# Two inverse square roots per pair of heads on POOL, as a power, in a one-core transformer kernel

## The reference

```python
kk = (k * k_k).reshape(hd)
kk = kk * lax.rsqrt(jnp.maximum(jnp.sum(kk * kk, axis=-1, keepdims=True), 1e-24))
...
y = rwkv7_scan(r, decay, k, v, -kk, kk * a)
mu = jnp.mean(y, axis=-1, keepdims=True)
var = jnp.mean(jnp.square(y - mu), axis=-1, keepdims=True)
y = ((y - mu) * lax.rsqrt(var + GN_EPS)).reshape(bsz, s, c) * gn_w + gn_b
```

## Time and profile before

| what | value |
|---|---|
| median of 3 runs | 2821.63 us |
| profiled execution, and its span | 2820.33 us, 2818.5 us |
| PE (TensorE) busy | 2771.2 us, 98% |
| DVE (VectorE) busy | 2023.7 us, 72% |
| ACT (ScalarE) busy | 1364.0 us, 48% |
| POOL (GpSimd) busy | 479.3 us, 17% |
| TensorE clock granted | full speed in all 40 slices |
| DMA busy share | 50.3% of 16 engines |

### The profile page before, as it was taken

How to read it: one execution, slowest core, us unless ns; L and a number is a source line. 1 busy time by engine, 2 the same in 40 slices (tenths; PEclk the granted TensorE clock), 3 DMA queues, 4 the chain that set the end, 5 groups by cost and what they waited for, 6 DMA issues and landing times.

```text
span 2818.5 us, 42260 instructions
## 1 busy us (share of the span) xinstructions
PE 2771.2 (98%) x16660; PEld 2434.1 (86%) x16660; DVE 2023.7 (72%) x3102; ACT 1364.0 (48%) x2051; POOL 479.3 (17%) x526
## 2 busy tenths in 40 slices
PE   8999999999999999999999999999999999999998
PEld 7888888888888888888888888878998888888887
DVE  7987797776776666656657888878677777667655
ACT  6453455455555445434435545434454444444434
POOL 2211011110111111001102635421111111001101
PEclk9999999999999999999999999999999999999999
DMA  6444333455555555555556534221365555555555
GB/s 227 162 160 159 121 116 132 145 191 188 193 187 190 192 191 191 192 190 193 188 183 199 177 124 133 92 76 53 120 202 191 191 192 189 193 188 194 189 180 164
DMA packets 133396, 474.65 MB, mean 168 GB/s; under 512 B 14800, under 2 KB 15056, under 8 KB 132944
## 3 DMA queue, kind: packets, MB, share of 16 engines
q1 hardware_dynamic: 133200, 471.96, 50.3%
HBM read 469.80 MB, written 2.10 MB: 167 GB/s over the span
## 4 chain that ended last, share of the span: by engine, by line
PE 90%; DVE 5%; ACT 2%; POOL 1%; issue 1%; DMA 0%; SPq 0%; DVEq 0%; ACTq 0%; POOLq 0%
PE ps L899 90%; DVE U L1869 1%; DVE ringl L1869 1%; POOL U L2551 1%; ACT high L1409 1%; PE ps L902 1%; POOL U L2624 0%; ACT U L1409 0%; DVE U L1878 0%; DVE xT L1869 0%; DMA xT<-in_x_dram 0%; DVE hx L1869 0%; DVE U L2067 0%; ACT hr L1409 0%; DVE U L1875 0%
## 5 line engine op out<-in xcount | busy, mean ns | idle before, releaser
L899 PE MATMUL ps<-hr,high 128*128 128x512 f32 x4672 | 1491.4, 397 | 11.8 <-DVE ringl L1869 10.8
L1869 DVE TENSOR_TENSOR ringl<-ring,high 128x1024 fp32r<-128x1024 f32 x888 | 1082.6, 1221 | 435.1 <-ACT high L1409 434.6
L1409 ACT ACTIVATE high<-ring 128x1024 fp32r<-128x1024 f32 x888 | 915.6, 1033 | 601.6 <-PE ps L899 590.7
L899 PEld LDWEIGHTS ps<-hr,ringl 128*128 128x128 f32 x4672 | 879.2, 188 | 192.5 <-issue 1.4
L899 PE MATMUL ps<-hr,ringl 128*128 128x256 f32 x4672 | 924.3, 279 | 0.0
L899 PEld LDWEIGHTS ps<-hr,high 128*128 128x128 f32 x4672 | 717.6, 188 | 21.0 <-issue 15.1
L899 PE MATMUL ps<-yur,high 128*128 128x512 f32 (+1 forms) x2432 | 682.9, 370 | 3.8 <-DVE xT L1869 2.2
L2551 POOL TENSOR_TENSOR U<-U,rs 128x256 f32<-128x256 f32 x292 | 264.5, 906 | 1688.3 <-DVE U L1869 1668.8
L899 PEld LDWEIGHTS ps<-yur,ringl 128*128 128x128 f32 x2176 | 400.0, 188 | 79.6
L1409 ACT ACTIVATE U<-ps 128x256 f32<-128x256 f32 (+3 forms) x481 | 172.8, 371 | 592.0 <-PE ps L899 567.6
L899 PE MATMUL ps<-yur,ringl 128*128 128x256 f32 x2176 | 429.9, 279 | 0.0
(11 more groups left out here) (178 smaller groups left out, 1250.2 us busy)
## 6 DMA issues: line engine op xcount, KB each, us to landing
ring<-in_w_dram SPq DMA_DIRECT2D x862, 512.0 KB, 3.3
ring<-in_w_dram SPq DMA_DIRECT2D x48, 256.0 KB, 3.3
xT<-in_x_dram SPq DMA_DIRECT2D x3, 512.0 KB, 8.1
out_dram<-hx SPq DMA_DIRECT2D x3, 512.0 KB, 2.7
cst<-in_cst_dram SPq DMA_DIRECT2D x1, 1374.5 KB, 12.5
yT<-in_lora_dram SPq DMA_DIRECT2D x1, 1024.0 KB, 7.4
xT<-in_x_dram SPq DMA_DIRECT2D x2, 256.0 KB, 4.5
U<-in_lora_dram SPq DMA_DIRECT2D x1, 512.0 KB, 5.4
```

Source lines behind the costliest of these rows:

```text
L899: return e.matmul(out, l, r, start=start, stop=stop)
L1409: return e.activation(out, i, ACT.Copy, scale=scale)
L1869: return e.tensor_tensor(out, a, b, op)
```

## The change

For each of the two normalisations, ACT's square root and DVE's reciprocal are replaced by one POOL operation that raises the tile to the power in a tile of constants, all minus one half (`mhalf`, 256 columns more in the constants). Ahead of the recurrence POOL takes what DVE has written after the maximum. Behind it ACT still moves the variance out of PSUM with scale and epsilon, as an Identity in place of the square root, since POOL's power reads SBUF. The steps `kk`, `nrm`, `var` and `fin` get other engines and assumed times in `RECUR`.

```diff
-         ("kk", ("PE", 0.45), ("DVE", 0.42), ("ACT", 1.7)), ("nrm", ("DVE", 3.1)), ...
+         ("kk", ("PE", 0.45), ("DVE", 0.42), ("POOL", 2.0)), ("nrm", ("DVE", 1.35)), ...
-       ... ("var", ("PE", 0.45), ("ACT", 1.8)), ("fin", ("DVE", 2.2), ("+POOL", 2.9))]
+       ... ("var", ("PE", 0.45), ("ACT", 0.45), ("POOL", 2.0)), ("fin", ("DVE", 0.45), ("+POOL", 2.9))]
# constants
+        ("mhalf", 256), ("zero", 128), ("causal", 128), ("causalT", 128),
# ACT, rwkv
-                    e.wait_ge(vc_.sem, vc_.after("kk2", q))
-                    e.activation(E, E, ACT.Sqrt).then_inc(ac.sem, ac.inc("rk", q))
-                    yield "kk"
...
-                    e.activation(rs, ps[b][:, 0:256], ACT.Sqrt, scale=1.0 / 64, bias=C("eps64"))\
+                    e.activation(rs, ps[b][:, 0:256], ACT.Identity, scale=1.0 / 64, bias=C("eps64"))\
# DVE, rwkv
-                    e.wait_ge(ac.sem, ac.after("rk", q))
-                    e.reciprocal(E, E).then_inc(vc_.sem, vc_.inc())
-                    e.wait_ge(vc_.sem, vc_.last())
+                    e.wait_ge(qc.sem, qc.after("ik", q))
                     tt(KK, KK, E, MUL).then_inc(vc_.sem, vc_.inc("nrm", q))
...
-                    e.wait_ge(ac.sem, ac.after("rs", q))
-                    e.reciprocal(rs, rs).then_inc(vc_.sem, vc_.inc())
-                    e.wait_ge(vc_.sem, vc_.last())
+                    e.wait_ge(qc.sem, qc.after("ir", q))
# POOL, rwkv, between "dec" and "fin"
+                    e.wait_ge(vc_.sem, vc_.after("kk2", q))
+                    tt(w["E"], w["E"], C("mhalf"), ALU.pow).then_inc(qc.sem, qc.inc("ik", q))
+                    yield "kk"
+                    rs = w["XT"].rearrange("p a b -> p (a b)")[:, 0:256]
+                    e.wait_ge(ract[s].sem, ract[s].after("rs", q))
+                    tt(rs, rs, C("mhalf"), ALU.pow).then_inc(qc.sem, qc.inc("ir", q))
+                    yield "var"
```

More of the change, by code:

```diff
@@ L49 @@
 RECUR = [("lw", ("PE", 1.75), ("DVE", 0.9), ("ACT", 2.4)), ("dec", ("DVE", 1.9), ("+POOL", 4.8), ("ACT", 0.4)),
-         ("kk", ("PE", 0.45), ("DVE", 0.42), ("ACT", 1.7)), ("nrm", ("DVE", 3.1)), ("em", ("DVE", 1.2)), ("exp", ("ACT", 2.9)),
+         ("kk", ("PE", 0.45), ("DVE", 0.42), ("POOL", 2.0)), ("nrm", ("DVE", 1.35)), ("em", ("DVE", 1.2)), ("exp", ("ACT", 2.9)),
          ("rk", ("PE", 0.45), ("DVE", 0.42)), ("ar", ("DVE", 1.8)), ("rows", ("PE", 0.9), ("ACT", 1.1)),
@@ L54 @@
        ("G1", ("PE", 0.7), ("ACT", 0.35)), ("sa1", ("PE", 0.45), ("ACT", 0.45)), ("o1", ("PE", 1.1), ("ACT", 0.35)),
-       ("mean", ("PE", 0.45), ("DVE", 0.45), ("ACT", 0.45)), ("var", ("PE", 0.45), ("ACT", 1.8)), ("fin", ("DVE", 2.2), ("+POOL", 2.9))]
+       ("mean", ("PE", 0.45), ("DVE", 0.45), ("ACT", 0.45)), ("var", ("PE", 0.45), ("ACT", 0.45), ("POOL", 2.0)), ("fin", ("DVE", 0.45), ("+POOL", 2.9))]
 ROPE1 = (("DVE", 2.9),)
@@ L74, in layout @@
         ("ones", 128), ("norm1", 16), ("eps", 1), ("ident", 128), ("bones", 128), ("SU", 128), ("utri", 128), ("MC", 4 * 64), ("B8", 128), ("E8", 8),
-        ("zero", 128), ("causal", 128), ("causalT", 128),
+        ("mhalf", 256), ("zero", 128), ("causal", 128), ("causalT", 128),
         ("head", 2), ("R2", 128), ("cos1", 256), ("sin1", 256), ("inv2", 1), ("cmpmask", 32), ("anyv", 2),
@@ L2743, in constants @@
     put("anyv", np.stack([i >= 31, i >= 0], 1).astype(np.float32))
+    put("mhalf", np.full((128, 256), -0.5, np.float32))
     put("eps", np.full((128, 1), EPS, np.float32))
```

## The result

The changed kernel takes 3442.78 us, the median of four runs (3439.72 to 3444.68), beside 2822.93 us for the kernel before (four runs, 2818.89 to 2824.79). The ratio is 1.2198, with a 95% interval of 1.218 to 1.2217: 22% slower, where 2818 us was forecast and the range ended at 2870. One number further down needs a word: of the two runs of the kernel with 20 us in its table one took 3515.68 us, at a granted clock of 0.805 over its span where the other had 0.921, and it is left out.

What follows compares the result with a forecast made beforehand. PE, busy 98% of the span, was taken to bound the kernel. From 2820.3 us, 4.5 of PE's waits went and 1.0 for later multiplies came: 2816.8, carried to the median 2818 us; range 2808 to 2870.

Steps and rivals of the forecast that it cites:

- The size of the power: Each of sixteen 128x256 powers on POOL was taken as 2.0 us, between 0.6 and 3.8 us.
- B: Slow power: DVE stands in order at 16 places and splits for PE are late; 2871 us at 7.6 us; chance 0.24.
- B1: The same DVE waiting in small, with a power of 3.8 to 6 us: 2839 us at 5 us; chance 0.14.
- 12 us for each microsecond: Kernel time lost per microsecond of power, between 2825 us at 3.8 and 2871 at 7.6.
- the quarter for the second power: Behind the recurrence, only a quarter of the second chain's delay was counted, 9 us at a power of 7.6 us.
- The gain of 4.5 us: Three waits of PE with removed work directly ahead should go: 1.61 + 1.59 + 1.31 us; bounds 0 and 13.8.
- the redrawn order moves them about, and I count on none of it: The other 9.3 us of PE's waits, for the triangular inverse and copies out of PSUM, were counted as no gain.
- the wait at the end of the recurrence: At 2006.77 PE waits 1.59 us for an evacuation behind the last reciprocal on DVE; it should vanish.
- the next from 1.31: At 2011.15 PE waits 1.31 us more in the same chain, from the last y to its halves; it should vanish.
- the one of 1.61 at 1963: At 1962.99 PE waits 1.61 us for an evacuation on ACT behind a table load and a square root; counted as gain.
- the ceiling of 13.8 us: Sum of PE's waits in the recurrence's stretch, 0.5% of the time: all that shorter DVE or ACT work can give back.
- The constants' DMA: At the start, 131 KB more of constants take 1.2 us more to transfer; costed at nothing, 1.2 us if wrong.

Runs made afterwards that it cites:

- the kernel with 20 us in its table: The changed kernel with 20.0 in place of 2.0 us for both powers in the table from which the order is drawn: 3326.34 us, by one run.
- 1.7 us at each place: The changed kernel, same order and table, with two products by a constant tile in place of each power: 2836.06 us, ratio 1.0045.
- one product at each place: The changed kernel with one product by a constant tile in place of each power: 2835.11 us; with 0.9 us in the table 2829.11, with the old durations 2842.26.

## Why the prediction was wrong, step by step

1. **The size of the power is the step that failed**: "POOL's longest operation of this shape, with two arithmetic steps, is nearest ... so I take 2.0 us", with 3.8 as the upper bound. It is 41.3 us, alone as well as in place, eleven times the bound. The bound came from DVE's ratio of a reciprocal to a two-input operation, two operations of another engine; nothing tied a power on POOL to it. The sentence that should have stopped me is in the prediction: no row shows a power. With no row, 3.8 wasn't a bound, and the range had nothing to hold it from above. I had one hint that 3.8 wasn't a bound, the count of the Trainium skill, GPSIMD Engine Reference, section 3.1 Elementwise, 3 operations a cycle at 1.2 GHz, and gave it weight in the chances of B and B1 alone. By it my estimate was 4.3 us, still about a tenth of the truth; turned round, 160 ns a column would be an estimate of 580 operations, where I had assumed 60. The run measures the duration only, so how the power is computed stays open. The stretch beside DVE's work, which I had as one more reason for 2.0, hardly matters: the mean is 41.285 us in the changed kernel, where DVE mostly stands still meanwhile, 41.356 in the kernel with 20 us in its table, where it waits less, and 41.26 alone.
2. **The mechanism of rival B is what happened**: DVE stands in order at 16 places until POOL has the power, and the splits for PE are late. It decides from about 3 us, as I had it. DVE's waits for POOL, to be 50 us and more in that case, are 611.5.
3. **Its price was too low.** I had 12 us for each microsecond; the runs show 16. At the true length my line would have given 2825 + 12 x 37.5 = 3275, with 16 it is 3425. What was off was mainly the quarter for the second power; alone it costs 325 us, and the first 336. The fall of the clock, with 40.5 us more of PE's busy time in the changed kernel, is part of these 16.
4. **The gain of 4.5 us didn't come, for another reason than the power.** With 1.7 us at each place, within my assumption of 2.0, the time is 2836, not 2818. This is the second step that failed: "the redrawn order moves them about, and I count on none of it". The redrawn order isn't neutral: with the operations held fixed (the inverse root on ACT) another redrawn order costs 14.7 us, and three orders of the changed kernel's queues, with one product at each place, lie at 2829, 2835 and 2842. How much of the 18 us is the order and how much POOL's place in the chain isn't separated. My forecast would have been wrong by 18 us even if the power's size had been right.
5. **Of the 4.5 us itself** the old order without reciprocals tells something. There the wait at the end of the recurrence shrinks from 1.59 to 0.60 us and the next from 1.31 to 0.99, but the one of 1.61 at 1963 remains (1.62). It stood behind a table load and a root on ACT, and both are still there in that kernel, so that term isn't tested by it. In sum PE's waits fall from 13.8 to 11.3 us by the waits' view, 2.5 us; the medians give 4.0, with an interval from 1.1 to 6.2. With the reciprocals gone from DVE (its busy time falls by 27.5 us) and nothing lost in exchange, this is what that part of the removed work was worth, well under the ceiling of 13.8 us. What the 28 table loads on ACT were worth no run shows by itself.
6. **Right**: the table loads fall to four in the stretch, ACT's busy time by 37.3 us, and DVE's by 21.6 (27.8 were removed, but DVE's 76 products of two SBUF tiles of 128x256 take 5.2 us longer in sum, 551 ns for 484 in the mean). Behind the last power's own wait, none at the `out1` blocks is over 1 us (0.6 four times, then 0.89). The constants' DMA takes 0.1 us longer, not 1.2, and costs nothing that shows: PE is busy 1566.57 us up to 1590, and 1566.42 with the old constants and the inverse root on ACT. In the kernel before it was 1567.37. Wrong: PE's waits in the stretch didn't fall from 13.8 to 10 us, its idle time rose to 595.5.

The inverse square root on ACT in the old order, at 2819.24 us, is the one version that beats both kernels, the kernel before by 0.13%. What isn't settled is whether an order drawn for the shorter DVE steps can be found that doesn't lose the 14.7 us; of four tables none did.

## What to carry to other kernels

An operation of which no row exists has no upper bound from rows of other operations; run it by itself before anything is built on it, which here takes one kernel. Where an engine works in order and the one that sets the time is fed by it, a wait beyond the slack of the order (here about 3 us) costs its full length at every place, however little the waiting step matters. And a change in a table from which an order is drawn is two changes: hold the order fixed in one run, and change the order alone in another, before the operation gets the credit or the blame.

## What the runs showed of the hardware that was unexpected

- A POOL power on two tiles of fp32 costs 160 ns a column (20.77 us for 128 columns, 41.26 for 256, 1.01 for 4), and doesn't depend on the number of partitions (41.23 with 16), nor, in what was tried, on the exponent (-0.5 or 2) or the data (a base of all ones).
- The granted clock of TensorE can stand at half with PE busy for 18.08 of 21 us (0.59 in the mean), in a stretch of small fp32 matmuls with short waits between, while 18.16 busy of the same 21 us in the kernel before, with main work among its matmuls, stood at 1.00. Part of the 18.08 us is the stretching by the clock itself.
- ACT's inverse square root takes what its root took: 418 ns from SBUF and 474 from PSUM for 128x256, beside 418 and 0.47 us, with a table load of 1283 ns ahead of each as before. It saves a reciprocal of 1.73 us on DVE.
